# A four-pass matmul trunk on one core: first loads and sums reordered, the MLP's input turned by VectorE, two sums moved to GpSimd

## What is computed

```python
hn = rms_norm(x, norm1_g)
z = gelu(hn @ a_w_in)                      # 1024 x 4096
u, v = split(z, 2)
v = layer_norm(v) * a_ln_g
sv = causal_ws_per_chunk(v) + a_bs         # 128-position chunks, 8 groups
x = x + (u * sv) @ a_w_out
x = x + square(relu(rms_norm(x, norm2_g) @ mlp_w1)) @ mlp_w2
out = rms_norm(x, final_g)
```

## Time and profile before

| | us |
|---|---|
| median of 3 runs | 1124.45 (1124.19 to 1124.59) |
| the profiled execution | 1126.03 |
| its span, first to last instruction | 1124.2 |
| PE / DVE / ACT / POOL busy | 1114.8 / 785.9 / 569.4 / 23.5 |
| HBM traffic | 172 GB/s over the span |

### The profile page before, as it was taken

The page is one execution under the profiler, slowest core; times in us unless marked ns, Lnnn a source line. Parts: engine busy times, 40 slices in busy tenths (PEclk is TensorE's granted clock), DMA queues, the critical chain, the costliest instruction groups (busy, mean ns, idle before and its releaser), DMA issues.

```text
span 1124.2 us, 13090 instructions
## 1 busy us (share of the span) xinstructions
PE 1114.8 (99%) x5088; PEld 928.2 (83%) x5088; DVE 785.9 (70%) x833; ACT 569.4 (51%) x870; POOL 23.5 (2%) x17
## 2 busy tenths in 40 slices
PE   8999999999999999999999999999999999999997
PEld 7888888888888888888888888888888888888886
DVE  4976655688779986678658547455599575677666
ACT  6774444553554334565774365454653433433456
POOL 0000000000000000000000000000000000000240
PEclk9999999999999999999999999999999999999999
DMA  8173253272865494731353635527878354343213
GB/s 294 45 210 127 94 187 113 75 244 93 316 250 221 159 358 144 217 113 38 113 187 126 211 113 183 193 108 272 293 292 305 111 226 187 113 150 113 78 73 150
DMA packets 81933, 193.80 MB, mean 172 GB/s; under 512 B 4528, under 2 KB 10704, under 8 KB 75216
## 3 DMA queue, kind: packets, MB, share of 16 engines
q1 hardware_dynamic: 81392, 192.69, 48.7%
q10 hardware_dynamic: 480, 0.28, 0.1%
HBM read 134.24 MB, written 58.72 MB: 172 GB/s over the span
## 4 chain that ended last, share of the span: by engine, by line
PE 98%; DMA 1%; ACT 0%; DVE 0%; ACTq 0%; issue 0%
PE banks L427 32%; PE banks L432 32%; PE banks L431 32%; PE banks L496 3%; PE banks L541 1%; DMA gain_rows<-in_a_ln_g_dram 1%; DVE rows L1516 0%; ACT spare L1133 0%; PE banks L503 0%; PE banks L552 0%; PE banks L523 0%; ACT rows L1325 0%; ACT o_rms L1333 0%; ACTq L922 0%; ACTq L924 0%
## 5 line engine op out<-in xcount | busy, mean ns | idle before, releaser
L984 ACT ACTIVATE pair_high<-left_and_right 128x1024 fp32r<-128x1024 f32 x168 | 177.2, 1060 | 244.4 <-PE banks L427 193.4
L1378 DVE TENSOR_TENSOR ring_low<-left_and_right,ring_high 128x512 fp32r<-128x512 f32 x224 | 152.6, 692 | 192.7 <-ACT ring_high L954 192.3
L1386 DVE TENSOR_TENSOR pair_low<-left_and_right,pair_high 128x1024 fp32r<-128x1024 f32 x168 | 204.1, 1230 | 113.9 <-ACT pair_high L984 113.9
L954 ACT ACTIVATE ring_high<-left_and_right 128x512 fp32r<-128x512 f32 x224 | 138.4, 629 | 251.2 <-PE banks L427 155.9
L427 PE MATMUL banks<-pair_high 128*128 128x512 f32 x672 | 261.9, 390 | 0.0
L432 PE MATMUL banks<-pair_high,pair_low 128*128 128x512 f32 x672 | 261.5, 389 | 0.0
L431 PE MATMUL banks<-pair_low,pair_high 128*128 128x512 f32 x672 | 261.4, 389 | 0.0
L427 PE MATMUL banks<-s_high,ring_high 128*128 128x512 f32 x384 | 149.6, 389 | 0.0
L431 PE MATMUL banks<-s_low,ring_high 128*128 128x512 f32 x384 | 149.4, 389 | 0.0
L432 PE MATMUL banks<-s_high,ring_low 128*128 128x512 f32 x384 | 149.4, 389 | 0.0
L427 PEld LDWEIGHTS banks<-pair_high 128*128 128x128 f32 x672 | 126.1, 188 | 26.6 <-DVE pair_low L1386 0.3
(11 more groups left out here) (116 smaller groups left out, 1223.5 us busy)
## 6 DMA issues: line engine op xcount, KB each, us to landing
left_and_right<-sums SPq DMA_DIRECT2D x40, 1024.0 KB, 7.1
left_and_right<-in_mlp_w_dram SPq DMA_DIRECT2D x36, 1024.0 KB, 6.5
sums<-rows SPq DMA_DIRECT2D x34, 1024.0 KB, 5.4
left_and_right<-in_a_w_in_dram SPq DMA_DIRECT2D x19, 1024.0 KB, 6.2
v_blocks<-rows SPq DMA_DIRECT2D x8, 1024.0 KB, 4.5
left_and_right<-in_a_w_out_dram SPq DMA_DIRECT2D x8, 1024.0 KB, 9.7
rows<-in_x_dram SPq DMA_DIRECT2D x7, 1024.0 KB, 8.7
spare<-v_blocks SPq DMA_DIRECT2D x6, 1024.0 KB, 6.9
```

Of the source, the lines that this page charges most:

```text
L954: nc.scalar.activation(ring_high[k][:, :], right_place(n, pos)[:, k, :], ACT.Copy)\
L984: nc.scalar.activation(pair_high[pair_entry(d, pos, k)][:, :, :], pair_of(d, pos, k), ACT.Copy)\
L1378: nc.vector.tensor_tensor(ring_low[k][:, :], right_place(n, pos)[:, k, :], ring_high[k][:, :].bitcast(F32), ALU.subtract).then_inc(low_don ...
L1386: nc.vector.tensor_tensor(pair_low[e][:, :, :], pair_of(d, pos, k), pair_high[e][:, :, :].bitcast(F32), ALU.subtract).then_inc(low_done, 1)
```

## The change

1. **Start.** Warm-up is four products ahead of g1's turn and two behind it; `turn_gains` and the three warm-ups behind it go. The second k-step of b11 gets a DMA of its own. The first unit runs as four high-by-high matmuls as soon as both high parts are there, then four with the low part of x, then four with the low part of the weights. b12 is loaded after b21. The layer norm's weight and g2 are loaded by SP after the first weights and turned in `single(1)`; the second copy of g2 goes.
2. **Sums of n = 0.** `sum_t(0,0)` moves on VectorE behind `sum_combo(0,"s2")`; `sum_t(0,2)` goes to GpSimd, ahead of the masking of ws.
3. **The MLP's input.** TensorE's 32 transposes and ScalarE's eight drains of a12 and a22 go. Both blocks are moved from SBUF to SBUF by 16 DMAs each (`move_quads`) and turned by VectorE; g2 is applied while the high and low parts and the sums s2 and s4 are made, in four steps each. `sum_combo(4,"s3")` goes to GpSimd. `add_rows(0,6)` moves ahead of the last two `split_low` of unit row (4,0).

```diff
 PE
-            warm(2 * WARM_UP)
+            warm(4)
             turn_g1()
+            warm(2)
             first_turn(0)
             first_turn(1)
-            turn_gains()
-            warm(3)
+            def first_unit():
+                pe.wait_ge(combo_high, 1)
+                pe.wait_ge(high_done, unit(0, 0, 0) + 1)
+                for m in range(4):
+                    (high by high)
+                pe.wait_ge(combo_low, 1)
+                for m in range(4):
+                    (low rows by high)
+                pe.wait_ge(low_done, unit(0, 0, 0) + 1)
+                for m in range(4):
+                    (high rows by low)
-                        if n == 4 and pos == 0 and k == 1:
-                            turn(4, "a22", set_of(slot(4, 1)))
-                        if d == 0 and pos == 6 and k == 5:
-                            turn(4, "a12", set_of(slot_double(0, 5)))
 SP
+            def move_quads(b, blk, dst):
+                y_final(sp, blk)
+                for q in range(4):
+                    for r in range(4):
+                        sp.dma_start(dst[32 * q:32 * q + 32, r:4 * QT:4, :],
+                                     block_of[blk][32 * r:32 * r + 32, :, P * q:P * q + P])\
+                          .then_inc(quads_landed[b], 16)
...
-                    load_quads("a21", "c22", quad)
-                    y_final(sp, "c11")
+                    load_quads("a21", "c22", quad_a21)
+                    sp.wait_ge(low_done, unit_double(0, 5, 7) + 1)
+                    move_quads("a12", "c11", quad_a12)
                     sp.dma_start(y_of("c11"), block_of["c11"]).then_inc(y_stored["c11"], 16)
                     sp.wait_ge(low_done, unit_double(0, 6, 3) + 1)
                     load_weight(4, "b12")
                     sp.wait_ge(low_done, unit_double(0, 6, 7) + 1)
                     load_weight(4, "b22")
-                    y_final(sp, "c21")
+                    move_quads("a22", "c21", quad_a22)
...
-            load(("b11", 0), quarter[0][:, 1:4, :], weight(0, "b11")[:, 1:4, :], quarter_landed[0], "quarter0")
+            sp.dma_start(quarter[0][:, 1:2, :], weight(0, "b11")[:, 1:2, :]).then_inc(second_landed, 16)
+            load(("b11", 0), quarter[0][:, 2:4, :], weight(0, "b11")[:, 2:4, :], quarter_landed[0], "quarter0")
             load_x("a12", 0, NB, NB)
-            load_weight(0, "b12")
             load_x("a21", 4, 0, NB)
             load_x("a22", 4, NB, NB)
             load_weight(0, "b21")
+            load_weight(0, "b12")
 ACT
+            def high_turned(s):
+                act.wait_ge(y_turned, {"a12": 3, "a22": 4}[s])
+                if s == "a12":
+                    act.wait_ge(unit_begun, done(unit_double(0, 6, 5)))
+                for k in range(4):
+                    nc.scalar.activation(high[s][:, k, :], raw_of[s][:, k, :], ACT.Copy,
+                                         scale=g2_fours[:, 0, k:k + 1]).then_inc(combo_high, 1)
 DVE
+            def sum_turned(s):
+                if s == "s2":
+                    dve.wait_ge(y_turned, 4)
+                    dve.wait_ge(s3_pooled, 1)
+                    out, left, right = raw_s2, raw_a22, raw_s3
...
                 if n == 0:
-                    sum_t(0, 0)
                     low_combo(0, "a12")
                     for k in range(4):
                         s3_rows(k)
                     split_low(0, 1, 0)
                     split_low(0, 1, 1)
                     sum_combo(0, "s2")
+                    sum_t(0, 0)
                     split_low(0, 1, 2)
                     split_low(0, 1, 3)
                 elif n == 4:
-                    add_rows(0, 6)
-                    low_combo(4, "a12")
+                    low_turned("a12")
                     sum_t(4, 0)
-                    split_low(4, 1, 0)
-                    split_low(4, 1, 1)
-                    sum_combo(4, "s2")
-                    split_low(4, 1, 2)
-                    split_low(4, 1, 3)
+                    for k in range(4):
+                        split_low(4, 1, k)
...
+                if n == 4:
+                    turn_y("a22")
+                    sum_turned("s2")
+                    low_step(4, "s2", 0)
                 split_low(n, 2, 0)
...
-                    sum_t(0, 2)
...
                     if pos == 6 and d == 0:
-                        sum_combo(4, "s3")
+                        turn_y("a12")
                     for k in range(4):
+                        if pos == 6 and d == 0 and k == 2:
+                            add_rows(0, 6)
 POOL
+            pool.wait_ge(*landed["b22", 0])
+            pool.wait_ge(t_summed, t_sum(0, 0))
+            nc.gpsimd.tensor_tensor(q["b12"], q["b22"], q["b12"], ALU.subtract).then_inc(t3_pooled, 1)
             pool.wait_ge(ws_landed, 16)
             nc.gpsimd.affine_select(...)
+            pool.wait_ge(y_scaled, 8)
+            nc.gpsimd.tensor_tensor(raw_s3[:, :, :], raw_a11[:, :, :], raw_a21[:, :, :], ALU.subtract)\
+              .then_inc(s3_pooled, 1)
```

More of the change, by code:

```diff
@@ L35 @@
 COMBOS = ["a12", "s2", "s1", "s3", "s4", "a22"]
+STEPPED = {0: [], 4: ["a11", "a12", "s2", "a22"]}
 REGIONS = ["a11", "a12", "a22", "s2", "s3", "s4", "s1"]
@@ L291, in trunk @@
         g2_landed = sem("g2_landed")
-        quads_landed = {b: sem(f"quads_landed_{b}") for b in ("a11", "a21", "a12")}
+        quads_landed = {b: sem(f"quads_landed_{b}") for b in ("a11", "a21", "a12", "a22")}
         y_turned = sem("y_turned")
         y_scaled = sem("y_scaled")
+        s3_pooled = sem("s3_pooled")
         v_stored = {b: sem(f"v_stored_{b}") for b in BLOCKS}
@@ L557, in single @@
                     for k in range(4):
-                        single_unit(n, pos, k)
+                        if n == 0 and pos == 0 and k == 0:
+                            first_unit()
+                        else:
+                            single_unit(n, pos, k)
                         if n == 0 and pos == 0 and k == 0:
@@ L562, in single @@
                         if n == 0 and pos == 0 and k > 0:
-                            turn(0, {1: "a12", 2: "a21", 3: "a22"}[k], set_of(1))
-                        if n == 4 and pos == 0 and k == 1:
-                            turn(4, "a22", set_of(slot(4, 1)))
+                            turn({1: "a12", 2: "a21", 3: "a22"}[k], set_of(1))
                         if pos == 2 and k == 2 and n == 1:
+                            turn_gains()
                             turn_ws()
@@ L1016, in scale_y @@
             def scale_y(blk):
-                i, raw = {"a11": (0, raw_a11), "a21": (1, raw_a21), "a12": (2, raw_a12)}[blk]
+                i, raw = {"a11": (0, raw_a11), "a21": (1, raw_a21)}[blk]
                 act.wait_ge(g2_landed, 16)
@@ L1149, in single @@
                 elif n == 4:
-                    high_combo(4, "a12")
+                    high_turned("a12")
                     split_high(4, 1, 0)
-                    evict_turned(4, "a22", set_of(slot(4, 1)))
                     split_high(4, 1, 1)
@@ L1272, in double @@
                         square_rows(0, "c11", y_sq, y_squared)
-                    if pos == 6 and d == 0:
-                        evict_turned(4, "a12", set_of(slot_double(0, 5)))
                     for k in range(4):
@@ L1454, in turn_y @@
             def turn_y(blk):
-                i, src, dst = {"a11": (0, quad_a11, raw_a11), "a21": (1, quad, raw_a21), "a12": (2, quad, raw_a12)}[blk]
-                dve.wait_ge(quads_landed[blk], 64)
+                src, dst = {"a11": (quad_a11, raw_a11), "a21": (quad_a21, raw_a21), "a12": (quad_a12, raw_a12),
+                            "a22": (quad_a22, raw_a22)}[blk]
+                dve.wait_ge(quads_landed[blk], 64 if blk in ("a11", "a21") else 256)
                 dve.wait_ge(low_done, unit_double(0, 3 if blk == "a12" else 4, 7) + 1)
@@ L1481, in sum_combo @@
                 nc.vector.tensor_tensor(*args).then_inc(combo_sum, 1)
+            def sum_turned(s):
+                if s == "s2":
+                    dve.wait_ge(y_turned, 4)
+                    dve.wait_ge(s3_pooled, 1)
+                    out, left, right = raw_s2, raw_a22, raw_s3
+                else:
+                    dve.wait_ge(combo_sum, combo_sum_count(4, "s1"))
+                    out, left, right = raw_s4, raw_a12, raw_s2
+                for k in range(4):
+                    nc.vector.scalar_tensor_tensor(out=out[:, k, :], in0=left[:, k, :], scalar=g2_fours[:, 0, k:k + 1],
+                                                   in1=right[:, k, :], op0=ALU.mult, op1=ALU.subtract)\
+                      .then_inc(combo_sum, 1)
             def add_block(n, blk):
@@ L1650, in single @@
                 split_low(n, 2, 2)
+                if n == 4:
+                    low_step(4, "s2", 3)
+                    sum_combo(4, "s1")
                 if summed:
@@ L1705, in single @@
                     low_combo(4, "s3")
[L1706 to L1707 removed]
+                if n == 0:
```

(9 more changed lines are left out.)

170 lines of the change are left out of this document (96 added, 74 removed).

## The result

| | before | after |
|---|---|---|
| median of the runs (four each, compared on one chip) | 1124.35 us (1124.19 to 1124.59) | 1133.51 us (1132.60 to 1134.57) |
| ratio, 95% interval | | 1.0081 [1.0065, 1.0097] |
| the profiled execution, its span | 1126.03, 1124.2 us | 1132.60, 1130.9 us |
| TensorE busy | 1114.8 us x5088 | 1114.0 us x5046 |
| GpSimd busy | 23.5 us | 32.5 us |

The change makes the kernel 0.8% slower. The forecast of 1130.2 had the sign and most of the mechanism, but the time lies 3.3 above it and 1.6 above the upper end of the range (1131.9).

A forecast was written before the change was run, and what follows sets the result against it. TensorE, busy 99% of the span, was taken as the bound. Start -2.5, n = 0 +5.5 and n = 4 +2.8 gave +5.8: profiled 1131.8, median 1130.2 us; main case 1126.7 to 1131.9, 8 in 10 1120.5 to 1131.9.

The forecast's parts named there:

- The offset of 1.6: Profiled execution to median: 1.6 taken off the profiled 1131.8, as for the kernel before, giving a median of 1130.2.
- The start: Warm-up and first unit: first matmul at 6.95 instead of 9.49, 2.5 us saved, with 0.8 and 3.3 as ends.
- the start does nothing: Rival at the start: the clock stays low for as much longer as the first product is earlier; 1132.8 us, chance 0.05.
- n = 0: First stage's sums: sum_t(0,0) ahead of a split costs 0.7, GpSimd's sum holding VectorE brings a 4.7 stall; 5.5 lost.
- n = 4: The MLP's input: 3.5 saved by removing transposes, 6.3 lost by what replaces them; 2.8 us lost.
- Step (a): Unit (0,6,7): GpSimd's s3 gets in while VectorE is idle and delays the low part; 2.0 us lost.
- Step (b): Unit (4,0,0): the turn of a12 stands on VectorE ahead of split_low(4,0,0); 2.3 us lost.
- Step (c): Pos 2 of single(4): VectorE's list from 509.4 delivers at 532.5, TensorE wants it at 531.2; 1.3 us lost.
- Step (d): Pos 3 of single(4): add_block and the low part of s1 arrive about 0.7 us late.
- the small DMAs are late: Rival at the MLP's input: c21's 16 DMAs land at 533, 9 behind turn_y's turn; +15, 1139 us, chance 0.05.
- VectorE isn't held: Rival at GpSimd's two sums: the exclusion doesn't strike them; -3.6, 1120.9 us, faster, chance 0.25.
- GpSimd stays out until add_block: Rival at n = 0: GpSimd gets in only near 44.5, about 1.2 lost there; +1.5, 1126.0 us, chance 0.17.

The follow-up runs named there:

- b_again: The kernel before, run and traced once more with no edit: 1125.07 us.
- e4: The kernel before with the new start alone, seven warm-ups ahead of g1's turn and three behind the first turns of x: 1124.33 us, ratio 0.9991.
- e3: The kernel before with the new start alone (warm-up, first unit, gains turned in single(1), split load of b11): 1124.46 us, ratio 0.9998.
- e1: The kernel after with sum_t(0,2) moved from GpSimd back to VectorE: 1129.90 us, ratio 1.0043.
- e5: The kernel after with sum_t(0,2) on VectorE, sum_t(0,0) and b12's load in their old places, the mask put off: 1127.95 us, ratio 1.0020.
- e2: The kernel after with GpSimd's s3 put off to run beside VectorE's turn of a12: 1131.59 us, ratio 1.0058.
- e6: e5 with s3 put off to the turn of a12, and that turn behind the first two splits of single(4): 1127.51 us, ratio 1.0017.
- e7: e5 with VectorE's turn of a22 replaced by a fill with zeros, its DMAs and their wait kept: 1126.22 us, ratio 1.0008.
- e8: e5 with e4's warm start, s3 beside the turn of a12, and a22 turned by 16 TensorE transposes: 1123.56 us, ratio 0.9991.
- e9: e8 with the splits of (4,0,0) to (4,0,3) and add_rows ahead of VectorE's turn of a12: 1123.72 us, ratio 0.9994.

## Why the prediction was right and wrong

**The offset of 1.6: wrong, and half of the miss.** The step that failed is "the execution before lies 1.6 above the median of the runs, so the median goes to 1130.2". b_again shows that such an offset is made at the start, above all by the first unit at half clock (5.20 against 3.63). The changed kernel has a new first unit, which ran at full clock in its trace. The prediction saw the low clock and even allowed 1.7 for it, and then took it off as if the changed kernel's execution would have it too. Without that subtraction the sum was 1131.8 for the profiled time, which came out at 1132.6. The rest of the 3.3: 0.8 in the terms below, and 0.9 by which the profiled execution after lies under the median of its own runs (1132.60 against 1133.51). In which stretch the other runs of the kernel after are longer was not traced.

That the terms add up to within 0.8 is in part luck. The start came out 1.2 better than its term, because of the clock; n = 0 came out 0.8 worse, n = 4 0.9 worse, and the gains turned in single(1), for which the sum has no term, cost 0.4.

The upper end of the main case doesn't follow from what is named for it: a start of 0.8 adds 1.7 and the mask up to 1, which gives 1132.9 and not 1131.9. The measured time lies above this as well.

**The start: mechanism right, size of -2.5 neither value.** Against the first trace it gave 3.72, beyond the end of 3.3, since both the first product and the first unit's clock gained. Against b_again it gives 1.73 in the kernel after, 0.9 in e4, and 0.0 in e3's trace, each ahead of pos 2. The rival "the start does nothing", held at 0.05, is a thing that happens in some executions.

**n = 0: right in kind, 5.5 forecast, 6.31 measured.** The exclusion is as the prediction took it from the output stage: 4.46 held, 4.6 forecast (of its three rests there, the one given as 1.12 is 1072.66 - 1071.58 = 1.08). Wrong was the place: GpSimd came in between the two splits, at 31.16, which have no gap between them, and not at the gap where 35.5 was forecast (31.8 with VectorE's own shift of 3.72). That moved the loss forward, to (0,1,3), but didn't change its sum. The 0.8 that was missing: the mask, 0.67 (named as "up to 1 more" and counted at nothing), and 0.18 from the split's end (42.05) to the matmul. e1 shows the first part at 3.8 in the trace, with the mask then moving to where it hurts, and e5 the whole.

The Trainium skill, SBUF — State Buffer, "Who interferes with whom", has the exclusion of VectorE's ops with two SBUF inputs; the runs agree with it in both directions, 4.79 for a subtraction of 1.22 and 3.91 for a transpose, with one input, of 3.83.

**n = 4: 6.3 lost forecast, 7.04 measured; 3.5 saved forecast, 3.34 measured.** Step (a), s3 beside the idle VectorE: 2.0 forecast, 1.93. e2 takes it away, 2.02. Step (b), the turn ahead of the first splits: 2.3 forecast, 2.32. Step (c), pos 2: 1.3 forecast, 2.31. Here three small things were missing. VectorE needed 0.4 more than the sum from its first split to the end of its list (15.8, from 511.75, against 15.4); the DMAs put the turn off by 0.24; and behind s2's steps TensorE was released by ScalarE's drain of a bank at 535.98 + 0.6 and not by the split at 535.58 + 0.6, so that it started 2.3 behind s2's last step where 1.9 was reckoned. Step (d): 0.7 forecast, 0.22.

**The small DMAs.** Forecast: sixteen issues at 0.48, the last at 520.1, four microseconds of cover. Measured: c21 is final at 515.4, the last issue is at 525.7, so (525.7 - 515.5)/15 = 0.68 each, and it lands 2.0 behind, at 527.7. VectorE wanted it 0.24 before it began at 527.79. The cover was used up; the price of 0.48 came from a row of four issues. The Trainium skill, DMA: Bandwidth & Descriptors, has the fixed cost of about 2 us per DMA in its section "Anatomy of one DMA — SWDGE (gpsimd) path", for DMAs issued by way of GpSimd. These go out from SP, and the trace has 2.0 from issue to landing (median), but the sixteen overlap, so that a block takes 12 and not 32. The rival "the small DMAs are late" (+15) did not come; in e6 a wait of 2.06 did.

**The rivals.** "VectorE isn't held" is refused by the rows of 5.06 and 4.79. "GpSimd stays out until add_block" is refused at 31.16. Why GpSimd came in here between two splits that follow each other without a gap, and in e1 with the mask between a sum and a split, and missed four such changes at 1060.52 stays open: no run varied it.

**The signs that the prediction gave.** The first product near 7, a stretched subtraction at both places (about 5; at n = 0 it is a split of 0.6 and not the sum of 2.3 that was to take nearly 7), no transposes in double(0) and the gaps of pos 0, 2 and 3 are all there. The silence of 4 to 5 us around 38 is not: it is three waits of 0.66, 1.96 and 1.35 with a unit at half clock between them.

## What to carry to other kernels

Before the time of a profiled execution is carried over to the median, find the unit in which it is longer than the others; if the change touches that unit, the offset goes with it. Work given to GpSimd is free only if VectorE has no two-input op due in all its length: put it beside a transpose, and count the next GpSimd op too. In a stage where VectorE's work already fills the time of the products, taking transposes from TensorE for VectorE paid them back one for one, in both orders that were tried, and a chain of small DMAs needs its whole length as cover, priced by as many issues as it has.

## What was not expected of the hardware

- A GpSimd sum of 2048 columns in 4.5 us gets in between two VectorE ops that follow each other without a gap (31.16); so does the mask, which reads one input only (31.0 in e1, held 0.9; 0.75 in b_again).
- Some of TensorE's waits of about 2 us were followed by 3.41 at the 1.2 GHz level (36.28 and 507.46 in the kernel after), and others were not (536.70 there, 2.15); in e6, where it waited 3.98, it was 6.83. Such a stretch cost nothing where another engine was late anyway (36.90 and 507.95 after), and where none was it cost 1.6 (e2, e7), and the longer one 2.7 (e6).
- The speed of the first unit is not certain: 5.39 in e3, 5.52 in e6 and 3.63 in the kernel after, with the same warm-up in all three. The kernel before, with its longer warm-up, has both as well (5.20 and 3.63). The three traces with the warm start (e4, e8, e9) have 3.62 to 3.64.
